# A two-layer decoder trunk in split float32: x ahead of the first weight and turned at once, splits and a table load reordered around the cycles and the merge, FOX's key in halves

## The reference

```python
for l in range(DEPTH):                                   # 2 layers
    h = rms_norm(x, norm_g[l])
    q_a, kv_a, g_a, z_a, q_b, k_b, v_b, f_b, z_b, merge = split(h @ w_in[l])
    y_a = nsa_mixer(q_a, kv_a, g_a, ...) * silu(z_a)     # 16 heads, 2 key groups
    y_b = fox_mixer(q_b, k_b, v_b, f_b, ...) * silu(z_b) # 16 heads, forgetting bias
    r_a, r_b = split(merge)
    merged = sigmoid(r_a) * (y_a @ w_proj_nsa[l]) + sigmoid(r_b) * (y_b @ w_proj_fox[l])
    x = x + merged @ w_out[l]
return rms_norm(x, final_g)
# nsa_mixer, compressed branch: 32-token blocks + pe -> silu(. @ w1) @ w2 gives k_cmp, v_cmp;
#   every head attends to them, to the selected blocks and to the window
```

## Time and profile before

| | |
|---|---|
| median of 3 runs | 1489.43 us (1489.36 to 1489.46) |
| the profiled execution's own time | 1489.96 us |
| its span, first to last instruction | 1487.9 us |
| granted TensorE clock, mean | 0.999 |
| instructions | 24906 |
| DMA | 117.85 MB, mean 79 GB/s |

### The profile page before, as it was taken

The page is one execution under the profiler, slowest core; times in us unless marked ns, Lnnn a source line. Parts: engine busy times, 40 slices in busy tenths (PEclk is TensorE's granted clock), DMA queues, the critical chain, the costliest instruction groups (busy, mean ns, idle before and its releaser), DMA issues.

```text
span 1487.9 us, 24906 instructions
## 1 busy us (share of the span) xinstructions
PE 1471.2 (99%) x7677; PEld 1241.0 (83%) x7677; DVE 1029.1 (69%) x2405; ACT 905.5 (61%) x1885; POOL 485.8 (33%) x578
## 2 busy tenths in 40 slices
PE   8999999999999999999999999999999999999998
PEld 7888888888888888888887888888888888888887
DVE  5887777778788874444558778788788787643444
ACT  5777777767777752223456777777777776422233
POOL 1436445445445410000024445445455363000000
PEclk9999999999999999999999999999999999999999
DMA  9222122222222143333462222222122222433332
GB/s 265 72 72 55 49 54 57 57 58 57 56 57 57 44 129 97 99 99 85 107 185 73 57 58 57 56 57 59 44 57 57 56 57 54 145 87 104 91 99 86
DMA packets 213891, 117.85 MB, mean 79 GB/s; under 512 B 9305, under 2 KB 212401, under 8 KB 213297
## 3 DMA queue, kind: packets, MB, share of 16 engines
q1 hardware_dynamic: 211408, 107.49, 27.1%
q0 software_dynamic: 1728, 8.66, 1.6%
q10 hardware_dynamic: 672, 0.70, 0.2%
HBM read 110.41 MB, written 6.42 MB: 79 GB/s over the span
## 4 chain that ended last, share of the span: by engine, by line
PE 89%; ACT 5%; DVE 3%; issue 1%; POOL 1%; DMA 0%; ACTq 0%; DVEq 0%; POOLq 0%
PE acc L1666 62%; PE o_pair L1744 8%; PE turned L1726 7%; PE scores L1718 4%; PE scores L1717 4%; ACT q_swap L765 1%; PE misc L1755 1%; ACT w_hi L735 1%; PE acc L1928 1%; DVE yt_lo L1504 1%; ACT kk_hi L803 1%; PE misc L1689 1%; PE o_pair L1770 1%; DVE w_lo L1113 0%; POOL q_swap L595 0%
## 5 line engine op out<-in xcount | busy, mean ns | idle before, releaser
L1666 PE MATMUL acc<-u_hi,w_hi 128*128 128x512 f32 x1104 | 436.6, 395 | 1.3 <-DVE w_lo L1113 0.8
L1666 PE MATMUL acc<-u_lo,w_hi 128*128 128x512 f32 x1104 | 435.0, 394 | 0.0
L1666 PE MATMUL acc<-u_hi,w_lo 128*128 128x512 f32 x1104 | 432.6, 394 | 0.0
L856 ACT ACTIVATE prob<-prob,row_max 128x128 f32<-128x128 f32 (+3 forms) x384 | 215.2, 560 | 182.0 <-DVE row_max L1280 180.0
L1113 DVE TENSOR_TENSOR w_lo<-w_raw,w_hi 128x1024 fp32r<-128x1024 f32 x188 | 234.8, 1249 | 83.5 <-ACT w_hi L735 81.8
L660 POOL TENSOR_SCALAR prob<-prob,row_inv,gates 128x128 f32<-128x128 f32 (+3 forms) x256 | 171.3, 669 | 328.6 <-DVE row_inv L1287 325.5
L735 ACT ACTIVATE w_hi<-w_raw 128x1024 fp32r<-128x1024 f32 x188 | 197.9, 1052 | 96.6 <-PE acc L1666 90.2
L1666 PEld LDWEIGHTS acc<-u_hi,w_hi 128*128 128x128 f32 x1104 | 207.4, 188 | 42.9 <-DVE u_lo L1131 2.0
L1666 PEld LDWEIGHTS acc<-u_hi,w_lo 128*128 128x128 f32 x1104 | 207.6, 188 | 38.9
L1666 PEld LDWEIGHTS acc<-u_lo,w_hi 128*128 128x128 f32 x1104 | 207.4, 188 | 37.3
L1280 DVE CUSTOM_DVE_ANT_0 prob<-scores,causal 128x128 f32<-128x128 f32 (+3 forms) x384 | 184.9, 482 | 45.2 <-PE scores L1718 34.7
(11 more groups left out here) (235 smaller groups left out, 2275.6 us busy)
## 6 DMA issues: line engine op xcount, KB each, us to landing
w_raw<-in_w_in_dram SPq DMA_DIRECT2D x140, 512.0 KB, 3.9
w_raw<-in_w_proj_nsa_dram SPq DMA_DIRECT2D x16, 512.0 KB, 3.9
w_raw<-in_w_proj_fox_dram SPq DMA_DIRECT2D x16, 512.0 KB, 4.0
w_raw<-in_w_out_dram SPq DMA_DIRECT2D x16, 512.0 KB, 4.0
x_scratch<-xT POOLq DMA_DIRECT2D x2, 2048.0 KB, 9.1
xT<-x_scratch POOLq DMA_DIRECT2D x2, 2048.0 KB, 8.3
x_nat<-in_x_dram SPq DMA_DIRECT2D x4, 512.0 KB, 6.8
c_w<-in_cmp_w_k_dram SPq DMA_DIRECT2D x4, 512.0 KB, 5.9
```

The source lines that it names most:

```text
L856: act.activation(prob[:, ring, 0:width], prob[:, ring, 0:width], ACT.Exp, bias=row_max[:, ring:ring + 1], scale=-1.0, accum_out=row_sum[:, ...
L1666: ins = pe.matmul((bank or acc[par])[0:width, :], w[:, par, k, 0:width], rhs, start=(n == 0), stop=(n == 23))
```

## The change

1. **Start.** SP issues x's first quarter ahead of the first weight. The 24 gain rows and the 64 place rows have semaphores of their own. TensorE turns the first block of x, then the 24 rows, then all of x, without the four later warm-up products, and only then does the first unit, unbroken; the place rows are turned behind it. ScalarE and VectorE follow with other orders; ScalarE issues the rope tables and biases behind its squares. The `w_hi` of unit 0 moves behind the first two `u_hi`.
2. **Ahead of the cycles.** ScalarE makes `w_hi` of unit 9 ahead of `kk_hi`. VectorE makes `z_silu` of unit 8 and `v_pair` ahead of `kk_lo`. The eight `vcb` operations go to slots 4 and 5 of the layer's first cycle; their source, the compressed values, is written by TensorE to `o_pair` and no longer to a `scores` bank, and the first product into `o_pair` waits for them. SP loads the weight of `kv(6)` two hidden weights earlier.
3. **FOX's key in halves**, last cycle of a layer: `kf_lo` of head 0 one slot earlier, on a new semaphore `kf_first`.
4. **The merge.** Of four `yt_lo` ahead of `m_th`, one stays; two follow behind it and one behind the next `w_lo`.
5. **The table load** moves behind the first `w_hi` of the output projection.

```diff
-            load(w_view, 0, *KV_UNITS[0], 0, 0)
             for n in range(4):
+                if n == 1:
+                    load(w_view, 0, *KV_UNITS[0], 0, 0)
                 ...
                 sp.dma_start(x_nat[:, :, cols], x[0].rearrange("(i p) d -> p i d", p=P)[:, :, cols]
                              ).then_inc(x_landed[n], 16)
...
+                        if h == 0 and rows == own(0):
+                            ins.then_inc(kf_first, 1)
...
                 swap_copy(l * 10 + 2, (2, 3), src=qk_raw)
+                split_hi(*kv(9))
                 k_round(q_rope, [(0, 1), (1, 1)], [(rope_done, l * 10 + 3)])
-                split_hi(*kv(9))
                 split_hi(*kv(10))
...
                 out0 = half0 + U_OUT // 2
-                table_of_sqrt()
...
                     split_hi(out0 + (k + 1) // 2, (k + 1) % 2)
                     if k:
                         normed(k - 1)
+                    else:
+                        table_of_sqrt()
...
-                at(plan.end[1] + (4 if cycle.last else 3), lambda: kf_rest(parts + 1))
+                if cycle.last:
+                    at(plan.end[1] + 3, lambda: kf_rest(parts + 1, (0,), nsa.m))
+                    at(plan.end[1] + 4, lambda: kf_rest(parts + 1, (1,)))
+                else:
+                    at(plan.end[1] + 3, lambda: kf_rest(parts + 1))
...
+                def vcb_upper():
+
+                    dve.wait_ge(c_out_mm, 2 * l + 2)
+                    for n in range(4):
+                        dve.tensor_scalar(vcb[N_PAD * n:N_PAD * n + N_PAD, :, n % 2, 0:HD], cv, 0.5, None,
+                                          ALU.mult).then_inc(cb_ready, 1)
...
                 if cycle.first:
+                    at(4, vcb_upper)
+                    at(5, vcb_lower)
...
                 split_lo(*kv(9))
-
+                v_of(*kv(8), z_silu[:, 1, :], [])
                 dve.wait_ge(pads, 2)
                 dve.wait_ge(c_out_mm, 2 * l + 1)
...
+                v_rest(l * 10, v_pair[:, :, 0, :, HD:2 * HD], v_pair[:, :, 0, :, 0:HD])
                 k_rest(q_rope, [(0, 1), (1, 1)], l * 26 + 2)
-                v_of(*kv(8), z_silu[:, 1, :], [])
-                v_rest(l * 10, v_pair[:, :, 0, :, HD:2 * HD], v_pair[:, :, 0, :, 0:HD])
                 split_lo(*kv(10))
...
-                yt_low(0, (0, 2, 4, 6))
+                yt_low(0, (0,))
                 gate_of(merge0 + 1, l, 1, 0)
+                yt_low(0, (2, 4))
                 split_lo(merge0 + 2, 0)
+                yt_low(0, (6,))
...
+                    if cycle.first and pair is nsa and a == 0:
+                        pe.wait_ge(cb_ready, CB_PARTS * (l + 1))
...
-                    pe.wait_ge(cb_ready, CB_PARTS * (l + 1))
+                    pe.wait_ge(cb_ready, CB_PARTS * l + 2)
...
-            pe.wait_ge(gains_landed, 16 * (DEPTH + 3))
-            pe.transpose(misc[:, 0:ROWS], gain_rows[:, :], ident[0:ROWS, 0:ROWS]
-                         ).then_inc(gains_turned, 1)
-            run_in(4)
...
+                if k == 0:
+                    pe.wait_ge(gains_landed, 16 * (DEPTH + 1))
+                    pe.transpose(misc[:, 0:GAINS], gain_rows[0:GAINS, :], ident[0:GAINS, 0:GAINS]
+                                 ).then_inc(gains_turned, 1)
+            unit_piece(0, 24, 0, 0, each_k=lambda n: (u_lo_done[n % 2], n // 2 + 1))
```

More of the change, by code:

```diff
@@ L291, in bass_trunk @@
         rope_landed = sem("rope_landed")
+        kf_first = sem("kf_first")
         gains_landed = sem("gains_landed")
+        places_landed = sem("places_landed")
+        places_turned = sem("places_turned")
+        places_done = sem("places_done")
         gains_turned = sem("gains_turned")
@@ L506, in _ @@
                 kv(5, free=2 * base + 4)
+                kv(6)
                 load_hidden(l, 1, w1_v)
                 load_second(l, 1, w2_v)
-                for n in range(6, len(KV_UNITS)):
+                for n in range(7, len(KV_UNITS)):
                     kv(n)
@@ L910, in _ @@
             for a, pe in ((0, pe_k), (1, pe_v)):
[L911 removed]
+                first = P - PLACES + a * DEPTH * CJ
                 act.dma_start(gain_rows[first:first + DEPTH * CJ, :], pe.rearrange("l (j a) d -> (l j) (a d)", a=2)
[L913 removed]
+                              ).then_inc(places_landed, 16)
             act.wait_ge(consts, 2)
             table_of_sqrt()
[L916 to L917 removed]
             for k in range(0, KT, 2):
@@ L924, in _ @@
                 u_high(0, k + 1)
+                if k == 0:
+                    split_hi(0, 0, wait=False)
             split_hi(0, 1, wait=False)
@@ L933, in _ @@
             gf_high(0)
+            for n in range(4):
+                act.wait_ge(x_landed[n], 16)
+            for qt in range(QT - 1):
+                act.activation(o_nat[:, qt, :], x_nat[:, qt, :], ACT.Square,
+                               accum_out=squared[:, qt:qt + 1]).then_inc(sq_summed, 1)
             for to, src in ((cosT[:, :], rope_c), (sinT[:, :], rope_s)):
@@ L1201, in qf_rest, with kf_rest @@
                 ins.then_inc(part_lo_done, 1)
-            def kf_rest(parts):
-                dve.wait_ge(part_hi_done, parts + 1)
-                for h in range(2):
+            def kf_rest(parts, heads=(0, 1), m=None):
+                if 1 in heads:
+                    dve.wait_ge(part_hi_done, parts + 1)
+                else:
+                    dve.wait_ge(kf_first, m + 1)
+                for h in heads:
                     ins = dve.tensor_tensor(kf_lo[own(h), h, :], qk_raw[own(h), :], kf_hi[own(h), h, :],
                                             ALU.subtract)
-                ins.then_inc(part_lo_done, 1)
+                if 1 in heads:
+                    ins.then_inc(part_lo_done, 1)
             def k_rest(src, places, parts):
@@ L1870, in _ @@
                 for g in range(GROUPS):
-                    ins = pe.matmul(scores[1][0:N_PAD, HD * g:HD * g + HD], c_hid[:, 1, N_PAD * g:N_PAD * g + N_PAD],
+                    ins = pe.matmul(o_pair[0:N_PAD, HD * g:HD * g + HD], c_hid[:, 1, N_PAD * g:N_PAD * g + N_PAD],
                                     c_w2[:, 1, :], start=True, stop=True)
```

77 lines of the change are left out of this document (41 added, 36 removed).

## The result

The changed kernel takes 1480.84 us, the median of four runs (1480.39 to 1481.20), against 1489.39 of the kernel before: ratio 0.9941, 95% interval 0.9929 to 0.9952. 1481.2 was forecast. The profiled execution took 1481.20 us (1489.96 before), its span is 1479.2 us. One execution of experiment 8 took 1808 us at a mean granted clock of 0.81 and is left out; all other times are of executions at 0.997 to 0.999. Each place of the kernel is compared by the starts of its products in the two timelines, from the end of the place before it on; the sum of the differences over the span is 8.7 us.

A forecast was written before the change was run, and what follows sets the result against it. TensorE, busy 99% of the span, was the bound, so only its idle time could be won: 3.0 + 4.2 - 2.1 + 0.9 + 0.9 + 1.3 = 8.2 us, giving 1481.2 us; 8-in-10 range 1478.4 to 1483.5.

The forecast's parts named there:

- The waits that were to go: TensorE's waits for v_pair and kf_lo would be gone, and those for w_lo nearly.
- the one that was to come: In each first cycle, a new TensorE wait for GpSimd's scaling at the turn formerly at 96.84, about 0.9 us long.
- step 1: Start: second unit starts at 19.3 instead of 22.36, 3.0 us won, bounds 1.0 and 3.5.
- rival E: Start: x's first two quarters land a microsecond later than before, giving 1482.2 us; chance 0.08.
- Rival C: Start: the clock rises late, say at 17 us, so the unit runs partly at half pace, 1483.0 us; chance 0.11.
- steps 2, 4, 6: Gains of 4.2 us ahead of the cycles, 0.9 from FOX's key in halves, 1.3 from moving the table load.
- my bound of 1.0: FOX's key in halves, last cycle: upper bound of the forecast gain of 0.9 us in two layers; lower bound 0.5.
- The margin of w_lo behind v_pair: Ahead of the cycles: this w_lo is 0.5 us from being late; if used up, up to 0.3 a layer returns.
- step 3: First cycle of each layer: the moved vcb operations cost 1.05 us a layer, 2.1 in all, ends 0 and 4.2.
- Paid once: First cycle: once TensorE is itself late the slack is back, so the 1.05 us a layer is lost only once.
- Rival B: First cycle: the loop passes all of vcb's delay on through several turns, 2.1 us a layer, 1483.3 us; chance 0.16.
- step 5: Ahead of the merge: one yt_lo behind w_lo makes w_lo 1.1 us earlier; 0.9 us won, bounds 0.5 and 0.95.

The follow-up runs named there:

- experiment 8: Changed kernel with the first weight behind x's second quarter: 1480.66 us; the filled kernel adds 8 warm-up products between the second and third quarter's turns: 1480.62 us.
- experiment 6: Changed kernel with the four upper vcb operations ahead of the cycles and the four lower ones in slot 7 instead of 5: 1478.44 us.
- experiment 7: Changed kernel with extra warm-up products between the turns of x's first and second quarter: 1482.25 us with 14, 1481.28 us with 8.
- experiment 3: Changed kernel with FOX's key whole, four yt_lo together and the table load ahead of w_hi, as before: 1484.53 us.
- experiment 5: Changed kernel with the four upper vcb operations moved from slot 4 to ahead of the cycles, the lower four still in slot 5: 1479.61 us.

## Why the prediction was right, and where its steps were off

The waits that were to go have gone, and the one that was to come stands at the turn that was named. The sum was 8.2 and the timelines give 8.7, with errors of both signs: the start 0.1 less than forecast, ahead of the cycles 0.55 more, the first cycles 0.56 less, FOX's key 0.36 and the table load 0.2 more. That the second and the third of these cancel is luck.

- **The start** (step 1). The second unit starts at 19.50, forecast 19.3, and this too is partly luck. x's second quarter landed 0.5 us late (9.05 for 8.54), half of what rival E had. Against that stands an error of my own: I took 0.77 us for a u_lo from two that took 1.63, but those two start at 14.89 and 15.76 with an operation of 0.75 each, so 0.13 us between them is idle; back to back they start 0.66 apart, before (20.05 and 20.72) as after. Over eight of them that is 0.9 too much. From the last u_lo to the next unit I had 0.9, and it is 1.26 in experiment 6 (17.63 to 18.89) and 1.39 here. The unit began at 13.65, not at 12.6: 0.4 of this is the last quarter, which landed at 12.11, and the rest its turns at the low clock. It then ran without a wait, so in the changed kernel TensorE itself is last, but by little: with 9.6 from the copy at 9.79 on, VectorE's chain allows 19.4 (experiment 7). In the filled kernel of experiment 8 it is the landing of the last quarter that binds.
- **The rule of the clock.** The sentence of the Trainium skill, page "TensorE: Matmul & The Clock Gate" (Part 1), that idle stretches bring the low clock back: the trace agrees in kind, with the fall to 0.50 behind 1.92 us of pause; the page asks for a longer idle stretch than that, and here the measurement decides. Rival C did not come about: the clock was high from 6.5 us on, fell at 10.0 and was back at 13.4, not at 17, so the turns did end at 13.7, as C has it, but none of the unit's products ran at half pace. In experiment 8 three did, and a gain of a microsecond was lost.
- **Ahead of the cycles, FOX, table** (steps 2, 4, 6). One term was mis-sized: a wait of x us makes the next 128x512 product x + 0.17 late, but the one behind that loses another 0.12 (experiment 3). With 0.29 in place of 0.17, w_lo's 2.4 us in six waits is 4.1 late instead of 3.4, and FOX's 0.6 in two is 1.2 (1.26 measured, beyond my bound of 1.0). v_pair's two waits of 1.26 cost 1.47 each. The margin of w_lo behind v_pair held.
- **The first cycle** (step 3) lost 2.7 instead of 2.1. Up to the turn of step 7 the reading held: the scaling for it ended 16.4 us behind the cycle's first turn instead of 14.3, so 2.1 us had gone on, and TensorE was 1.09 late there, forecast 1.05. As 0.34 of that had fallen at step 5 already, where pt_lo of step 3 came late, the wait in the list is 0.51 and not 0.9. "Paid once" is what failed: behind step 7 came another 0.24 a layer, up to step 14, and experiment 5 has as much there with half of the work. The longer scaling of step 4 was not in the prediction at all; it just fitted into the slack. Rival B had the direction, and a price that was too high: 2.1 us a layer against 1.33.
- **The merge** (step 5) is as forecast, 0.94, through two errors. At the waiting product and the one behind it 0.57 a layer are won, which is the 1.2 of the corrected lateness; in layer 0, 0.2 of it goes 5 us later, where the next w_lo is late behind its weight (experiment 8).

## What to carry to other kernels

Work that is moved off a waiting engine's path should go to a row where the receiving engine idles, and not to one where it merely has a low busy share: four operations of 1.2 us cost nothing, 0.50 or 0.83 us in three slots of the same cycle. Slack is read at each step behind the new place, and idle time counts only if it lies behind the inserted work. Look also at what the moved work pushes another engine's operation into: here 1.2 us of it made a scaling on GpSimd 1 us longer. Price a wait with what the next instruction loses too, here 0.29 us on top of each at products of 128x512 and 0.2 to 0.35 at the others.

## What the runs showed of the hardware

- At the start of the kernel pauses of 1.4, 1.5, 1.7, 1.8, 1.9 and 2.5 us between turns were followed, at once or eight turns later, by turns 213 ns apart and a granted clock of 0.50 for over 3 us; pauses of 0.8, 1.0 and 1.2 us were not.
- The clock rose in the middle of transposes (at 13.4 us in the changed kernel), and transposes run at both paces: 213 and 109 ns from start to start.
- A warm-up product of 128x128 in float32 is recorded as two products; a filling of 14 takes 3.1 us, not 1.5.
- A scaling of 128x128 on GpSimd that begins within a w_lo of VectorE takes 1.3 to 1.5 us (16 in the changed kernel), any other 0.45 to 0.61 (80). The two w_lo of the first cycles that it fell into took 1.43 us instead of 1.24. That the two engines hold each other up is read from these rows; no run tests it.
- The same transfer order gives other landings from one execution to the next: x's second quarter at 8.5 to 9.4 us. That is as large as the effects that were tested at the start, and only the timeline tells them apart.
